# Attention in a hybrid transformer trunk: transposes ahead of the filler, values one step earlier, outputs in another PSUM bank

## The reference

```python
def one_block(qblk):
    s = jnp.einsum('bqhgd,bshd->bhgqs', qblk.astype(jnp.float32), kf) * scale
    pr = jax.nn.softmax(s, axis=-1)
    return jnp.einsum('bhgqs,bshe->bqhge', pr, vf).astype(q.dtype)

mla_k = jnp.concatenate([fc['mla_k'], fl['mla_k']], axis=1)   # latent rows see context and latent
y_mla = block_attention(fl['mla_q'][:, :, :, None, :], mla_k, mla_v, mla_scale)
y_gqa = block_attention(fl['gqa_q'].reshape(B, L, GQA_KV_HEADS, G, GQA_HD), gqa_k, gqa_v, gqa_scale)
```

## The kernel before

| step | layer 0 MLA | layer 0 GQA | layer 1 MLA | layer 1 GQA |
|---|---|---|---|---|
| 0 | next query, 12 matmuls | query, 24 | query, 6 | query, 24 of 512 |
| 1 | 48 | 24 | 24 of 512 | 24 of 512 |
| 2 | 24 | 24, column sums | 48, then k, 12 | column sums, 12 of 512 |
| 3 | 24 | 24 | V | 12 of 512 |
| 4 | k, 12 | 24 | | |
| 5 | V | 24 | | |

## Time and profile before

### The profile page before, as it was taken

One profiled execution on the slowest core, in us unless ns is written; L12 is line 12 of the kernel. 1 busy time (PEld: TensorE's weight loads), 2 busy tenths in 40 slices (PEclk: granted clock), 3 DMA queues, 4 the chain that ended last, 5 costly groups with the idle time before them and its releaser, 6 DMA issues.

```text
span 3528.8 us, 49714 instructions
## 1 busy us (share of the span) xinstructions
PE 3240.0 (92%) x18760; PEld 2735.5 (78%) x18760; DVE 1519.6 (43%) x2047; ACT 1254.8 (36%) x1777; POOL 397.4 (11%) x304
## 2 busy tenths in 40 slices
PE   6999999999898889999999978998999898889998
PEld 5788877888777777788888867877777776668886
DVE  4555424445335533422222355553455445443333
ACT  3344432454333332211211234444355433432222
POOL 0011100111101201000100101110011101011001
PEclk9999999999999999999999999999999999999999
DMA  4222141111331143123142432222221232222222
GB/s 181 78 71 73 64 136 63 60 54 59 101 121 64 42 137 126 48 96 112 64 135 70 140 111 81 75 82 84 75 71 65 75 115 68 90 100 95 95 95 101
DMA packets 100921, 315.17 MB, mean 89 GB/s; under 512 B 11088, under 2 KB 21456, under 8 KB 100816
## 3 DMA queue, kind: packets, MB, share of 16 engines
q1 hardware_dynamic: 55872, 202.40, 17.2%
q10 hardware_dynamic: 44944, 111.32, 9.4%
HBM read 283.79 MB, written 29.88 MB: 89 GB/s over the span
## 4 chain that ended last, share of the span: by engine, by line
PE 45%; issue 8%; DVE 5%; ACT 2%; POOL 1%; DMA 1%; ACTq 0%; DVEq 0%; POOLq 0%
PE ps L1417 43%; PE ps L1531 1%; POOL ptl L1399 1%; DVE mx L927 1%; ACT wh L431 1%; PE ps L1509 1%; DVE wl L896 1%; DVE ptl L945 0%; DMA mraw<-in_wmod 0%; DVE tmp L906 0%; DVE tmp L1061 0%; DVE tmp L966 0%; ACT pth L484 0%; PE ps L1441 0%; ACT side L509 0%
## 5 line engine op out<-in xcount | busy, mean ns | idle before, releaser
L1417 PE MATMUL ps<-hh,wh 128*128 128x512 f32 x2768 | 827.2, 359 | 48.5 <-DVE wl L896 25.8
L1417 PE MATMUL ps<-hl,wh 128*128 128x512 f32 x2768 | 818.8, 356 | 0.0
L1417 PE MATMUL ps<-hh,wl 128*128 128x512 f32 x2768 | 815.5, 355 | 0.0
L896 DVE TENSOR_TENSOR wl<-raw,wh 128x1024 fp32r<-128x1024 f32 x364 | 484.1, 1330 | 645.6 <-ACT wh L431 616.1
L1417 PEld LDWEIGHTS ps<-hh,wh 128*128 128x128 f32 x2768 | 454.9, 191 | 138.3 <-issue 48.6
L1417 PEld LDWEIGHTS ps<-hh,wl 128*128 128x128 f32 x2768 | 455.6, 191 | 78.3
L1417 PEld LDWEIGHTS ps<-hl,wh 128*128 128x128 f32 x2768 | 455.0, 191 | 73.8 <-issue 0.7
L431 ACT ACTIVATE wh<-raw 128x1024 fp32r<-128x1024 f32 x364 | 382.5, 1051 | 228.7 <-PE ps L1417 193.2
L1417 PE MATMUL ps<-yh,wh 128*128 128x512 f32 (+1 forms) x1296 | 412.0, 372 | 27.5 <-DVE wl L896 15.1
L1417 PE MATMUL ps<-yl,wh 128*128 128x512 f32 (+1 forms) x1296 | 398.3, 362 | 0.0
L1417 PE MATMUL ps<-yh,wl 128*128 128x512 f32 (+1 forms) x1296 | 397.4, 361 | 0.0
(11 more groups left out here) (190 smaller groups left out, 3452.5 us busy)
## 6 DMA issues: line engine op xcount, KB each, us to landing
raw<-in_stream SPq DMA_DIRECT2D x364, 512.0 KB, 3.5
mraw<-in_wmod ACTq DMA_DIRECT2D x40, 512.0 KB, 3.5
prob<-in_wmod ACTq DMA_DIRECT2D x40, 512.0 KB, 3.5
gspill<-prob ACTq DMA_DIRECT2D x32, 384.0 KB, 2.3
tmp<-gspill ACTq DMA_DIRECT2D x24, 384.0 KB, 3.1
early_y<-in_wmod SPq DMA_DIRECT2D x12, 512.0 KB, 14.6
vraw<-gspill ACTq DMA_DIRECT2D x16, 384.0 KB, 3.5
dec<-in_dec ACTq DMA_DIRECT2D x8, 768.0 KB, 4.2
```

The source lines that it names most:

```text
L896: dve.tensor_tensor(wl[:, s, :], raw[:, s, :], wh[:, s, :].bitcast(F32), ALU.subtract).then_inc(sem("w_lo"), 1)
L1417: ins = pe.matmul(out, lhs[w], rhs[x](cols), start=start and n == 0, stop=stop and n == 2)
```

## The change

The steps are put in another order on three engines, and two regions of PSUM change places.

- TensorE: scores, transposes of tile `n - 2`, `fill(n)`, and in **odd** steps values of the tiles `n - 3` and `n - 2`. The values of a pair so come one step earlier.
- ScalarE: `t_hi` of tile `n - 2` first, then exp, `fill(n)`, and `y_hi` in even steps as before. VectorE: maximum, reciprocal, `t_lo`, `fill(n)`, and `y_lo` in even steps.
- `OUTS` moves to bank 7 (odd scores), `QSUM` to bank 5 (even scores). Scores of the steps 1 and 3 now wait for `y_lo`, of the output two and one pairs back, where those of 0 and 2 did; values wait for the exp of an odd step.
- In GQA the column sums, the rotation and the root move from step 2 to step `gqa_stat`: 3 in layer 0, 1 in layer 1. The query's halves follow one step after that.
- The lags of the `y` semaphores fall from 2 to 1. In the first head's lone filler the column sums still stand behind the raw projection of step 1 in the queue of TensorE.

```diff
-LAG = {"s_rinv": 1, "s_pn": 1, "t_ready": 2, "t_hi": 2, "t_lo": 2, "y_ready": 2, "y_hi": 2, "y_lo": 2}
+LAG = {"s_rinv": 1, "s_pn": 1, "t_ready": 2, "t_hi": 2, "t_lo": 2, "y_ready": 1, "y_hi": 1, "y_lo": 1}
...
+def gqa_stat(nq):
+
+    return nq - 3
...
-        OUTS = SCORES[0] + TOK
-        QSUM = SCORES[1] + TOK
+        OUTS = SCORES[1] + TOK
+        QSUM = SCORES[0] + TOK
...
                 for n in range(c.steps(last)):
+                    m = n - 2
+                    if c.has(m):
+                        st = c.span(m)
+                        act.wait_ge(sem("t_ready"), c.v("t_ready", m))
+                        act.activation(pth[:, 0:st, (m % 2) * P:(m % 2) * P + P],
+                                       ps[:, TRANS:TRANS + st * P].rearrange("p (s q) -> p s q", q=P),
+                                       ACT.Copy).then_inc(sem("t_hi"), 1)
                     if n < c.nq:
...
                     fill(n)
                     if n % 2 == 0 and c.has(n - 3):
                         y_hi(c, n // 2 - 2, home)
-                    m = n - 2
-                    if c.has(m):
-                        st = c.span(m)
-                        act.wait_ge(sem("t_ready"), c.v("t_ready", m))
-                        act.activation(pth[:, 0:st, (m % 2) * P:(m % 2) * P + P],
-                                       ps[:, TRANS:TRANS + st * P].rearrange("p (s q) -> p s q", q=P),
-                                       ACT.Copy).then_inc(sem("t_hi"), 1)
...
-                    if query and n == 2:
+                    if query and n == gqa_stat(nt // P):
...
-                    if query and n == 3:
+                    if query and n == gqa_stat(nt // P) + 1:
...
-                    fill(n)
-                    if n % 2 == 0 and c.has(n - 3):
-                        y_lo(c, n // 2 - 2, home)
                     m = n - 2
...
                                           pth[:, 0:st, cols].bitcast(F32), ALU.subtract).then_inc(sem("t_lo"), 1)
+                    fill(n)
+                    if n % 2 == 0 and c.has(n - 3):
+                        y_lo(c, n // 2 - 2, home)
...
-                        if n in (0, 2) and c.has(n - 5):
-                            pe.wait_ge(sem("y_lo"), c.v("y_lo", n // 2 - 3))
-
-                        if n == 3 and std is not None:
+                        if n in (1, 3) and c.has(n - 5):
+                            pe.wait_ge(sem("y_lo"), c.v("y_lo", (n - 5) // 2))
+
+                        if n == 2 and c.nq == 4 and std is not None:
                             pe.wait_ge(sem("v_std"), std)
...
-                    if n == 2:
-
-                        pe.wait_ge(sem("s_exp"), c.v("s_exp", 1))
-                    fill(n)
-                    if n % 2 == 0 and c.has(n - 3):
-                        values(c, n, par if n >= 3 else 1 - par)
                     m = n - 2
...
                         ins.then_inc(sem("t_ready"), 1)
+                    if n == gqa_stat(c.nq):
+                        pe.wait_ge(sem("s_exp"), c.v("s_exp", n - 1))
+                    fill(n)
+                    if n % 2 and c.has(n - 2):
+                        values(c, n, par if n >= 3 else 1 - par)
 
             def values(c, n, vpar):
-                m = n - 3
+                m = n - 2
...
-                pe.wait_ge(sem("s_exp"), c.v("s_exp", min(n, 2)))
+                pe.wait_ge(sem("s_exp"), c.v("s_exp", min(n, 3)))
                 if c.has(m - 2):
-                    pe.wait_ge(sem("y_lo"), c.v("y_lo", n // 2 - 3))
+                    pe.wait_ge(sem("y_lo"), c.v("y_lo", (n - 5) // 2))
```

More of the change, by code:

```diff
@@ L1013, in fill @@
                             split(at, c0 + query + j + 1)
-                    if query and n == 2:
+                    if query and n == gqa_stat(nq):
                         dve.wait_ge(sem("free0"), at.v("free0", f0 + 1))
@@ L1018, in fill @@
                         sine(at, kq, 0)
-                    if query and n == 3:
+                    if query and n == gqa_stat(nq) + 1:
                         dve.wait_ge(sem("v_std"), at.v("v_std", kq + 1))
@@ L1592, in gqa_query, with raw @@
                 qs, pieces = gqa_steps(nt // P, raws, alone)
+                def raw(n):
+                    for j, steps in enumerate(pieces):
+                        if alone and n == steps[0] and j == 0:
+                            pe.wait_ge(sem("vt_lo"), at.v("vt_lo"))
+                        gate(at, c0 + query + j, j if alone else f0 + query + j, steps, n, nt, 1 - j if alone else 0)
                 def fill(n):
@@ L1596, in fill @@
                         gate(at, c0, f0, qs, n, nt)
-                    if query and n == 2:
+                    if alone and n == 1:
+                        raw(n)
+                    if query and n == gqa_stat(nt // P):
                         pe.wait_ge(sem("free0"), at.v("free0", f0 + 1))
@@ L1602, in fill @@
                         ins.then_inc(sem("v_stat"), 1)
[L1603 to L1606, removed]
+                    if not alone or n != 1:
+                        raw(n)
                 return fill
```

## The result

| | us |
|---|---|
| before, median of 4 runs | 3530.35 (3522.54 to 3536.19) |
| after, median of 4 runs | 3665.69 (3653.42 to 3676.31) |
| ratio | 1.0384 [1.0342, 1.0426] |
| forecast | 3645 (3590 to 3680) |

The change makes the kernel 3.8% slower, 135 us by the medians, on the side and inside the range that the prediction gave. The profiled execution after is the quickest of the four: 3653.42 us, 122.5 above the profiled one of before.

The account below looks back on a forecast made before the run. The prediction took TensorE's own queue as the bound. To the profiled 3531 us it added 79 for new waits net of the idle time removed and 36 for lost clock: 3646, say 3645 us, range 3590 to 3680.

Parts of the forecast that it names:

- filler of 12 matmuls too short in step 0: Layer 0 MLA, step 0: TensorE done at 2.3 us, `y_lo` only at 5.15, so scores wait 2.9 us.
- k's copies and `wl` ahead of `y_lo` in step 2 of layer 1's MLA: Copies of k and `wl` come before `y_lo` after k's projection, with nothing filling TensorE: wait 3.75 us a head.
- the long chain of GQA's step 2: Layer 1 GQA: table load, exp, weight split, query scale and low half precede `y_lo`, done at 9.1 us: wait 5.8 us.
- V behind `kl`: MLA: V's projection waits for the bank that k's copies free, 1.2 us a head in layer 0, 1.3 in layer 1.
- idles of up to 1.4 us cost nothing of the clock: Short TensorE idles, as in layer 1's MLA before, leave the granted clock at 1.00, so they were priced at zero.
- the scale of the query 1.46: Layer 1 GQA, step 2: VectorE's scaling of the query, ahead of `y_lo`, was taken to last 1.46 us.
- I take all of the 66 us as gone: All TensorE idle time over bare work in the 24 looped heads, 66 us, was assumed removed by the new order.
- rival (C): The evacuation always lands before the filler ends, so only removed waits count: 3531 - 66 = 3465 us; chance 0.05.
- layer 0 MLA one near 2.6 (1.0 a head), layer 1 MLA two above 3 (3.3): New long TensorE idles per head and their clock cost in us, within a clock term of +36 us for all heads.
- (A): Waits come as worked out but the clock holds: 3531 + 79 = 3610 us; chance 0.27.
- (B): Only step 2's evacuations bind, ScalarE reaching step 0's earlier: +21 us, clock 20, total 3572 us; chance 0.08.
- (D): Waits and gains cancel, leaving the whole kernel within 0.5% of before; chance 0.03.

Follow-up runs that it names:

- the first experiment: Changed kernel with both output evacuations, `y_hi` and `y_lo`, moved to the head of their even step, ahead of maximum and exp: 3493.21 us, ratio 0.9884.
- with step 2 moved: Changed kernel with `y_hi` and `y_lo` at the head of steps 2 and 4 only, step 0 left as it was: 3564.71 us, ratio 1.0107.
- both later moves: Added to both evacuations at the head: next query's `wh` ahead of exp (3476.93 us), then layer 1 GQA's query halves back in step 3 (3471.34 us).

## Why the prediction was right

**The mechanism.** The waits stand where they were foretold, with the releaser that was named, twice a head, and moving the two evacuations takes away all of them. Layer 1's GQA no longer waits for the query's low half, either (`yl` is the only releaser that the waits view of its weight loads has there). Six other steps of the argument held too: filler of 12 matmuls too short in step 0, k's copies and `wl` ahead of `y_lo` in step 2 of layer 1's MLA, the long chain of GQA's step 2, small waits in layer 0's GQA, V behind `kl`, and a clock that falls in layer 1's MLA most. One did not: that idles of up to 1.4 us cost nothing of the clock.

**The sum.** The prediction compared new heads without clock loss with old heads that hold some (0.4 and 1.0 us in the GQA stages), so its terms are put here as written and sorted anew by the table of heads above. In us, for 24 heads, around the profiled execution:

| term | as written | sorted anew | measured |
|---|---|---|---|
| net work and waits | +79 | +88 | +71 |
| clock | +36 | +33 | +55 |
| first and last heads, the rest | 0 | 0 | -3 |
| total | +115 | +121 | +122.5 |

That the total came so near is in part luck: two terms were off by 17 and 22 us, in opposite directions.

The 6 us between 115 and 121 are a slip: the 1.0 us a head that layer 1's GQA paid for its clock before ("of which 1.0 is paid now") was inside the 32.28 us already, and taken off a second time.

*Waits, 17 too many.* Nine of them lie in layer 1's GQA (1.5 us a head), and some seven of these are one instruction: "the scale of the query 1.46". It took 0.17, and the wait of step 3 was 4.7 us where 5.8 was put. That row was taken under a GpSimd multiplication, and in the new order this is over when the scale runs. The rest is 0.2 to 0.6 us a head in the other stages; in layer 0's GQA, the 0.5 us "for VectorE" before the last values did not come.

*The idle time removed, "I take all of the 66 us as gone".* In the changed kernel this held: besides `yl`, the waits view has only the 1.1 us a head before V's projection in layer 0's MLA (1.2 was put) and 1.4 in layer 1's (1.3 was put). But part of it was only hidden behind the waits for `yl`. With these taken away, MLA heads hold 2.7 and 3.1 us over their bare work (40.5 net and 35.5 against 37.8 and 32.4), GQA 0.1 and 1.9. The waits for `wl`, 1.1 us a head in both MLA stages, and for exp, 2.1 in layer 1's GQA, come to light, and I had seen neither. This is why rival (C)'s 3465 was too low.

*The clock, 22 too few.* This is the term that was mis-sized: "layer 0 MLA one near 2.6 (1.0 a head), layer 1 MLA two above 3 (3.3)". Measured were 3.2 and 5.0, and 2.3 in layer 1's GQA where 2.65 was put. I took the price of an idle of 2.4 us from layer 1's GQA before (1.0 a head), and nothing for idles of up to 1.4.

In layer 0's MLA of the changed kernel, both were too low. The granted clock fell to 0.50 behind each of the six idles of 2.8 us, at 1.7 us apiece. It fell three times more, and for longer, 2 to 3 us after the wait of 1.1 us for the copies of k was over. Three windows of the changed kernel: between that wait and the fall, the fall, and the fall behind the 2.79 us shown above.

```profile
308.70:311.10 2.40, 2.40 (x22) 2.40 (x22) 2.37 (x6) 1.21 (x3) 0.24 (x1) 1.00 0.11 14
311.20:318.00 6.80, 6.80 (x34) 6.80 (x34) 1.39 (x2) 0.92 (x3) 0.27 (x1) 0.50 0.18 70
...
324.90:328.20 3.30, 3.30 (x13) 2.91 (x12) 2.30 (x5) 1.57 (x4) 1.07 (x1) 0.50 0.46 151
```

Half of 6.8 us is 3.4, so the three cost 10 us, half of this stage's loss. The kernel that keeps TensorE busy in its waits has two of the same kind, and they are all of its loss in layer 0's MLA:

```profile
264.60:271.40 6.80, 6.80 (x34) 6.80 (x33) 1.57 (x2) 1.10 (x3) 0.45 (x1) 0.50 0.22 75
```

The kernel before had no wait there, and 1.00. Nor does a long idle always bring a fall: with step 2 moved, three of the six idles of 2.8 us did. In layer 1's MLA the changed kernel has eleven falls, and two of them, of 14 and 17 us, make half of the stage's loss. Length alone does not give the price; what decides it is open.

By whole runs the clock's part can be seen without any window: the profiled execution of before is 3530.96 at 0.967, a loss of 117 us; the four of after lose from 172 (3653.42 at 0.953) to 199 (3676.31 at 0.946), so 55 to 82 more; the term's upper bound, twice 36, was a little short. The spread of the changed kernel's times is that of its clock.

The Trainium skill, "TensorE: Matmul & The Clock Gate", Part 1, has the array fall to the lower of two rates after idleness. By that rule, the trace agrees for the long idles: those of 2.8 us in the changed kernel were followed by 0.50, and layer 1's heads hold 1.00 with TensorE kept busy. The falls behind a wait of 1.1 us, in stages at 0.97 and 0.99, are not foretold by it.

**The rivals.** (A), the clock holds, is out by the 0.89 to 0.94 of three stages; its 3610 is nearly the 3595 of the kernel that keeps TensorE busy. (B), only step 2 binds, is out: six of twelve waits are those of step 0, and moving them alone is worth 92 us. (C), the evacuation always lands in time, is what the first experiment made true by moving it; that came to 3493, not the 3465 of the sum, by the idle time that stayed. It took both later moves to get to 3471. (D), gains and waits cancel, is out with the ratio. The chances listed outside the range 3590 to 3680 add up to 0.23, not 0.2.

**Not settled.** What lets the clock fall behind a short wait, and which part of the 1.2% comes from transposes ahead of the filler and which from values a step earlier. Transposes ahead of the filler with values left where they were needs a third slot of `pth` and `ptl`, and this was not tried.

## What to carry to other kernels

When a PSUM bank changes its partner, work out for each new pair of writer and reader what stands in the reader's engine queue ahead of the copy that frees it; an evacuation whose data is ready belongs at the head of the step, and here its place was worth 172 us, from 3.8% slower to 1.2% faster. Price an idle of TensorE twice, once for its length and once for the clock. Here the second was nothing for waits of 1.5 us a head, 2.3 for 7.3, 3.2 for 4.2 and 5.0 for 7.2, and it differs from run to run. Taking away a wait can bring to light others that stood behind it. Before taking a duration from a row, look at what the other engines did in that moment.

## What the runs showed of the hardware

A VectorE instruction on 4 columns took as long as the GpSimd one beside it. In the kernel before, start 0.03 us after GpSimd's multiplication and end 0.02 us behind it; the timeline of GpSimd:

```profile
2666.35 1.47 POOL L1352 TENSOR_TENSOR prob<-prob,ri 128x768 f32<-128x768 f32 x1 [6.93 <-DVE ri L936]
```

The same form of instruction took 0.17 us in the changed kernel with GpSimd idle. Not every VectorE instruction is held up: in the chain of step 3 above, `ptl` (one input from PSUM) took its 0.96 us although GpSimd was at work, by its timeline:

```profile
2758.22 1.47 POOL L1357 TENSOR_TENSOR prob<-prob,ri 128x768 f32<-128x768 f32 x1 [8.76 <-DVE ri L941]
```

The first product of the rotation moved under GpSimd's multiplication by the change, and the means of its group, before and after, are

```profile
L959 DVE TENSOR_TENSOR tmp<-tmp,rope 64x512 f32<-64x512 f32 x18 | 12.4, 690 | 2.2 <-ACT tmp L525 1.7
```

```profile
L964 DVE TENSOR_TENSOR tmp<-tmp,rope 64x512 f32<-64x512 f32 x18 | 18.9, 1048 | 2.2 <-ACT tmp L530 1.7
```

In the changed kernel's timeline such a product starts at 279.67, 0.27 us after a GpSimd multiplication of 1.47 us, and takes 1.74.

The Trainium skill, "SBUF — State Buffer", section "SBUF: two separate sides", describes a port pair that VectorE and GpSimd take in turn, each for a whole instruction, and which VectorE needs for some forms only. The runs agree, the 1298 and 191 ns above with them.
